# Reordered evacuations, swapped probability buffers, a longer output tail and a moved remainder in a streamed four-layer trunk

## The reference

```
score = where(adm, sum_h w_h * relu(qi_h . ki), -inf);  idx = top_k(score, n_sel)
logits = q . k[idx] * HEAD_DIM**-0.5 + bias;  out = softmax(logits) . v[idx] @ w_o
# recurrent block
y = gelu(xn @ w_y + b_y);  xc = causal_dwconv(xn @ w_x + b_x) + conv_b
r, ig = sigmoid(xc @ w_r + b_r), sigmoid(xc @ w_i + b_i);  a = exp(-8 * r * softplus(-lam))
h_t = a_t * h_{t-1} + sqrt(1 - a_t**2) * ig * xc;  out = (h * y) @ w_out + b_out
# every layer, and one last norm
x = x + mixer(rmsnorm(x));  x = x + swiglu(rmsnorm(x))
```

## Time and profile before

| | |
|---|---|
| median of 3 executions | 1799.42 us (1798.11 to 1799.64) |
| the profiled execution | 1799.41 us, its span 1797.6 us |
| mean granted TensorE clock | 0.994 |
| PE busy | 1773.3 us (99%) |
| DVE, ACT, POOL busy | 1068.2 us (59%), 715.7 us (40%), 223.6 us (12%) |
| DMA | 216.96 MB, 121 GB/s |

### The profile page before, as it was taken

One profiled execution on the slowest core, in us unless ns is written; L12 is line 12 of the kernel. 1 busy time (PEld: TensorE's weight loads), 2 busy tenths in 40 slices (PEclk: granted clock), 3 DMA queues, 4 the chain that ended last, 5 costly groups with the idle time before them and its releaser, 6 DMA issues.

```text
span 1797.6 us, 27817 instructions
## 1 busy us (share of the span) xinstructions
PE 1773.3 (99%) x10014; PEld 1736.3 (97%) x10014; DVE 1068.2 (59%) x1848; ACT 715.7 (40%) x1139; POOL 223.6 (12%) x266
## 2 busy tenths in 40 slices
PE   9999999999999999999999999999999999999997
PEld 8988999999999999999999999999999889999997
DVE  7976855544587755554476655554458756555533
ACT  5366433333368433333222343333323554333331
POOL 5000300001235400001100200000140004000010
PEclk9999999999999999999999999999999999999998
DMA  8311333333333433334433333333454113433341
GB/s 304 121 36 60 111 123 122 123 119 128 122 111 106 132 129 118 124 114 136 139 117 117 119 118 125 121 124 120 136 187 161 48 48 95 133 132 118 129 141 59
DMA packets 63844, 216.96 MB, mean 121 GB/s; under 512 B 7153, under 2 KB 8769, under 8 KB 63521
## 3 DMA queue, kind: packets, MB, share of 16 engines
q1 hardware_dynamic: 59520, 202.25, 34.1%
q0 software_dynamic: 3280, 12.12, 2.2%
q10 hardware_dynamic: 976, 1.70, 0.3%
HBM read 212.38 MB, written 3.66 MB: 120 GB/s over the span
## 4 chain that ended last, share of the span: by engine, by line
PE 90%; DVE 6%; ACT 3%; issue 1%; DMA 0%; DVEq 0%; ACTq 0%
PE bank L705 26%; PE bank L704 26%; PE bank L703 26%; DVE w_lo L1308 2%; PE bank L903 1%; PE bank L859 1%; PE bank L880 1%; PE bank L861 1%; PE bank L860 1%; PE bank L922 1%; ACT w_hi L1026 1%; PE bank L886 1%; DVE work_b L1465 0%; DVE cv L1641 0%; PE bank L929 0%
## 5 line engine op out<-in xcount | busy, mean ns | idle before, releaser
L1308 DVE TENSOR_TENSOR w_lo<-raw,w_hi 128x1024 fp32r<-128x1024 f32 x382 | 490.4, 1288 | 312.3 <-ACT w_hi L1026 310.7
L703 PE MATMUL bank<-a_hi,w_hi 128*128 128x400 f32 (+2 forms) x1936 | 673.3, 348 | 1.1 <-DVE w_lo L1308 1.1
L704 PE MATMUL bank<-a_lo,w_hi 128*128 128x400 f32 (+2 forms) x1936 | 666.0, 344 | 0.0
L705 PE MATMUL bank<-a_hi,w_lo 128*128 128x400 f32 (+2 forms) x1936 | 665.3, 344 | 0.0
L1026 ACT ACTIVATE w_hi<-raw 128x1024 fp32r<-128x1024 f32 x382 | 399.9, 1052 | 345.7 <-PE bank L705 339.2
L703 PEld LDWEIGHTS bank<-a_hi,w_hi 128*128 128x128 f32 (+1 forms) x1936 | 362.5, 187 | 5.2 <-issue 1.2
L705 PEld LDWEIGHTS bank<-a_hi,w_lo 128*128 128x128 f32 (+1 forms) x1936 | 364.8, 188 | 0.6
L704 PEld LDWEIGHTS bank<-a_lo,w_hi 128*128 128x128 f32 (+1 forms) x1936 | 362.7, 187 | 2.6
L705 PE MATMUL bank<-h_hi,w_lo 128*128 128x400 f32 (+1 forms) x704 | 240.8, 342 | 0.0
L704 PE MATMUL bank<-h_lo,w_hi 128*128 128x400 f32 (+1 forms) x704 | 240.1, 341 | 0.0
L703 PE MATMUL bank<-h_hi,w_hi 128*128 128x400 f32 (+1 forms) x704 | 239.2, 340 | 0.0
(11 more groups left out here) (251 smaller groups left out, 1770.3 us busy)
## 6 DMA issues: line engine op xcount, KB each, us to landing
raw<-in_w_all SPq DMA_DIRECT2D x382, 512.0 KB, 3.5
bias_p<-rel_scratch POOLq DMA_DIRECT2D x2, 2176.0 KB, 11.0
k_s<-in_ck_t POOLq DMA_DIRECT2D x4, 512.0 KB, 8.6
v_c<-in_cv POOLq DMA_DIRECT2D x2, 1024.0 KB, 15.9
ki_s<-in_cki_t POOLq DMA_DIRECT2D x4, 256.0 KB, 5.4
x<-in_x_t SPq DMA_DIRECT2D x2, 400.0 KB, 6.4
x<-in_x_t ACTq DMA_DIRECT2D x2, 400.0 KB, 6.9
out_v_t<-v_f POOLq DMA_DIRECT2D x2, 400.0 KB, 5.0
```

What stands on the lines that cost most here:

```text
L703: pe.matmul(out, wh, hi[:, kc, c0:T], start=(first and n == 0), stop=False)
L704: pe.matmul(out, wh, lo[:, kc, c0:T], start=False, stop=False)
L705: mm = pe.matmul(out, wl, hi[:, kc, c0:T], start=False, stop=(last and n == len(blocks) - 1))
L1308: nc.vector.tensor_tensor(w_lo[:, s, :], raw[:, s, :], w_hi[:, s, :].bitcast(F32), ALU.subtract).then_inc(lo_ready, 1)
```

## The change

Six edits:

1. Where an attention core begins, DVE does `queries_out(2)` right behind `values_out`, then two `take(1)` in place of three, then `queries_out(3)`. The `split` for u0+12, the third `take(1)` and `mask_made(1)` move into the loop (steps 0, 2 and 3), and the rounds of `take(2)` and `mask_made(2)` come one step later.
2. `buffer_of` swaps the two probability buffers of gp = 1 (and in both cores the first group of gp = 1 now gets buffer 0), and ACT waits for u0+17 only where it writes buffer 1.
3. `WO_TAIL` is 9 and no longer 6: nine blocks of w_o stand behind the last step. The other 23 are spread over the same steps as 26 were.
4. In the recurrent layer the eight `low` move from POOL to DVE.
5. POOL's remaining `tap`s stand one behind the other.
6. `TAIL_BUSY`: five matmuls of 128 columns, of which nothing is read, stand ahead of each `last_sq` wait at the end.

```diff
-WO_TAIL = 6
+WO_TAIL = 9
+def buffer_of(a, g):
+    return (g - len(GROUPS[a]) // 2 * GROUPS[a][g][0][1]) % 2
@@ PE, values; ACT, the copy to pt
-                    p = pt[gp][g % 2]
+                    p = pt[gp][buffer_of(a, g)]
-                    if gp:
+                    if gp and buffer_of(a, g):
                         act.wait_ge(unit_used, u0 + 17)
@@ PE, the end (twice, ahead of last_sq 1 and of last_sq 2)
+            for _ in range(TAIL_BUSY):
+                pe.matmul(bank[7][:, 0:128], ones[:], ones[:], start=True, stop=True)
@@ DVE, ahead of the core's loop
                 values_out()
-                for _ in range(3):
+                queries_out(2, done(11))
+                for _ in range(2):
                     take(1)
-                mask_made(1)
-                queries_out(2, done(11))
-                split(None, 0, u0 + 12 + AHEAD)
                 queries_out(3, done(12))
@@ DVE, in the loop
                     if n < N_IT[a]:
                         reduced(n)
+                    if n == 0:
+                        split(None, 0, u0 + 12 + AHEAD)
...
-                    if n in (3, 5, 7, 9, 11):
+                    if n == 2:
+                        take(1)
+                    if n == 3:
+                        mask_made(1)
+                    if n in (4, 6, 8, 10, 12):
                         take(2)
-                    if n == 12:
+                    if n == 13:
                         mask_made(2)
@@ POOL, recurrent
-                for what, m in [(tap, 0), (tap, 1), (tap, 2), (low, 0), (tap, 3), (low, 1), (tap, 4), (low, 2), (tap, 5), (low, 3),
-                                (low, 4), (tap, 6), (low, 5), (restart, 0), (tap, 7), (restart, 1), (low, 6), (low, 7),
-                                (restart, 2), (restart, 3)] + [(scale, m) for m in range(4)]:
+                for what, m in [(tap, m) for m in range(7)] + [(restart, 0), (tap, 7), (restart, 1), (restart, 2), (restart, 3)] + [
+                                (scale, m) for m in range(4)]:
@@ DVE, recurrent (low as on POOL before)
-                behind = [[], [(taps, 0)], [(taps, 1)], [(taps, 2)], [(taps, 3)], [(taps, 4)], [(taps, 5)], [],
-                          [(taps, 6), (rest, 0)], [(taps, 7), (rest, 1)], [(rest, 2)], [(rest, 3)], [(recur, 0)],
+                behind = [[], [(taps, 0)], [(taps, 1)], [(low, 0), (taps, 2)], [(low, 1), (taps, 3)], [(low, 2), (taps, 4)],
+                          [(low, 3), (taps, 5)], [(low, 4)], [(low, 5), (taps, 6), (rest, 0)], [(taps, 7), (rest, 1)],
+                          [(low, 6), (rest, 2)], [(low, 7), (rest, 3)], [(recur, 0)],
```

More of the change, by code:

```diff
@@ L72, in rec_unit @@
     return k, sum(1 for kd, _ in REC[:k] if kd != "g")
-WARM_UP = 24
+WARM_UP, TAIL_BUSY = 24, 5
 (P_NMIX, P_NFFN, P_NFIN, P_BY, P_BX, P_CW, P_CB, P_BR, P_BI, P_LAM, P_BO, P_CC) = (
@@ L593, in tap @@
                                        ALU.mult, ALU.add).then_inc(tap_ready, 1)
-                def low(m):
-                    pool.wait_ge(conv_hi, m + 1)
-                    pool.tensor_tensor(b_lo[:, m, :], xc[:, m, :], b_hi[:, m, :].bitcast(F32), ALU.subtract).then_inc(xc_fed, 1)
                 def restart(m):
@@ L1135, in copies @@
                     slot = n - (LAST[a][g] - len(GROUPS[a][g]) + 1)
-                    p, ps = pt[gp][g % 2], bank[4 + k % 2]
+                    p, ps = pt[gp][buffer_of(a, g)], bank[4 + k % 2]
                     act.wait_ge(tr_done, UB[a] + k + 1)
@@ L1674, in merged_low, with low @@
                     nc.vector.tensor_tensor(b_lo[:, m, :], y_b[:, m, :], b_hi[:, m, :].bitcast(F32), ALU.subtract).then_inc(fed, 1)
-                behind = [[], [(taps, 0)], [(taps, 1)], [(taps, 2)], [(taps, 3)], [(taps, 4)], [(taps, 5)], [],
-                          [(taps, 6), (rest, 0)], [(taps, 7), (rest, 1)], [(rest, 2)], [(rest, 3)], [(recur, 0)],
+                def low(m):
+                    dve.wait_ge(conv_hi, m + 1)
+                    nc.vector.tensor_tensor(b_lo[:, m, :], xc[:, m, :], b_hi[:, m, :].bitcast(F32), ALU.subtract).then_inc(xc_fed, 1)
+                behind = [[], [(taps, 0)], [(taps, 1)], [(low, 0), (taps, 2)], [(low, 1), (taps, 3)], [(low, 2), (taps, 4)],
+                          [(low, 3), (taps, 5)], [(low, 4)], [(low, 5), (taps, 6), (rest, 0)], [(taps, 7), (rest, 1)],
+                          [(low, 6), (rest, 2)], [(low, 7), (rest, 3)], [(recur, 0)],
                           [(recur, 2), (rest, 4), (rest, 5)], [], [(rest, 6), (rest, 7)],
```

## The result

The changed kernel takes 1787.91 us (median of 5 executions, 1787.87 to 1789.58); 1788.3 was forecast. The kernel before took 1798.11, 1798.18, 1799.42 and 1799.64 us in the same series, and once 2925.82, an execution that nothing on record explains and that is left out here. Against 1799.42, the median that the forecast started from, the gain is 11.5 us; against 1798.80, the median of the four, it is 10.9. The ratio on record is 0.9941, with an interval of 0.9925 to 0.9957.

The account below looks back on a forecast made before the run. PE bounds the kernel, busy 1773.3 of 1797.6 us, plus its idle places and clock losses. Gains 0.8 + 1.8 + 1.4 + 4.6 + 1.7 + 0 + 0.8 = 11.1 us from 1799.4 give 1788.3 us, range 1785.0 to 1794.5.

Parts of the forecast that it names:

- The rule of the Trainium skill that spoke against the edit: Recurrent layer: `low` on DVE would meet POOL's `cv`; four stretched cost 3.2 us more, a loss of about 1.5.
- the debt: Attention cores' beginnings: moved take, mask and w_lo, 2.5 us of DVE work, expected to eat about one microsecond in layer 0.
- Beginnings: Starts of both attention cores, evacuations first: gain 0.8 us in layer 0 and 1.8 in layer 3.
- the lead: Attention cores' beginnings: `logits(1)` comes 1.75 us earlier because `queries_out(3)` starts when PE delivers.
- Buffers: Second half of heads, swapped probability buffers: gain 1.4 us in layer 0 and 4.6 in layer 3.
- the nine blocks: Cores' ends: three more kept blocks cover nothing, gain 0, bounds -0.5 and 2.4; rival that they cover, chance 0.03.
- Recurrent layer: `low` moved to DVE: chain 1.72 us earlier, half clock behind the gates gone, output product wait grows; gain 1.7 us.
- End: Program's end: busy matmuls hold the clock, last pair takes half its 1.65 us; gain 0.8 us.
- The first, a fall behind the output product: Rival: the clock falls at the recurrent layer's longer second stall; price 1.5 us, 1789.8 us, chance 0.25.
- the x phase was relieved: Rival said not: recurrent layer's line 1645 stays at 1.13 us, DVE has 1.96 more; 1792.0 to 1793.2 us, chance 0.06.
- the debt didn't eat the lead: Rival said it would: moved work eats the whole lead in both cores; price 0.8 + 1.8, 1790.9 us, chance 0.13.
- the w_lo of u0+23: Rival: 6.4 us later in each core, it delays the ring's loads; 12.8 us, to 1801.1 us, chance 0.03.

Follow-up runs that it names:

- edit 2 alone: The kernel before with only the swapped probability buffers of gp = 1, ACT waiting for u0+17 only at buffer 1: 1792.25 us, ratio 0.9965.
- edit 6 alone: The kernel before with only the two sets of five busy matmuls at the end: 1797.12 us, ratio 0.9994.
- the runs with single edits: The kernel before with some edits only: edit 1 1795.24 us, edit 2 1792.25, edits 4 and 5 1796.98, edit 6 1797.12.
- edit 1: The kernel before with only the evacuations moved ahead of the top-k where the attention cores begin: 1795.24 us, ratio 0.9982.

## Why the steps held

**POOL beside DVE.** The changed kernel, with a subtraction on POOL that nobody reads, in the places that `low` had there.

```diff
+                def beside(m):
+                    pool.wait_ge(conv_hi, m + 1)
...
+                    pool.tensor_tensor(sq[:], xe[:, m, 0:T], xe[:, m, 4:T + 4], ALU.subtract).then_inc(beside_done, 1)
...
-                for what, m in [(tap, m) for m in range(7)] + [(restart, 0), (tap, 7), ...
+                for what, m in [(tap, 0), (tap, 1), (tap, 2), (beside, 0), (tap, 3), (beside, 1), (tap, 4), (beside, 2), (tap, 5),
+                                (beside, 3), (beside, 4), (tap, 6)] + [(restart, 0), (tap, 7), ...
```

> The changed kernel, but POOL does a subtraction of two SBUF inputs of 400 columns for each of x tiles 0 to 4 where it did the low half before; nobody reads the result. Theory: the last convolution step on DVE was slow because it ran beside POOL's instruction with two inputs; it goes back from 0.35 to about 1.1 us in five units, a unit of DVE takes 4.57 + 0.8 = 5.4 us, and PE's wait at the gates grows by some 3 us: 1790.5 to 1792.5 us. Rival: the step was slow because it read and wrote xc while POOL read the same tile; POOL's instruction here reads xe alone, so the step stays at 0.35 and the time at 1787.9 us.

Measured: 1790.29 us (1790.19 to 1790.48), 2.3 us more than the changed kernel. One unit on DVE in the changed kernel, with the same pair in an earlier unit, where POOL's `cv` doesn't run beside it, and then the same unit of this one with POOL's row:

```profile
494.17 1.34 DVE L1647 SCALAR_TENSOR_TENSOR cv<-xe,par,cv 128x424 f32<-128x424 f32 x2
...
501.13 1.22 DVE L1310 TENSOR_TENSOR w_lo<-raw,w_hi 128x1024 fp32r<-128x1024 f32 x1
...
502.81 0.57 DVE L1686 TENSOR_TENSOR b_lo<-xc,b_hi 128x400 fp32r<-128x400 f32 x1
503.29 1.70 DVE L1647 SCALAR_TENSOR_TENSOR cv<-xe,par,cv 128x424 f32<-128x424 f32 x2
505.03 0.50 DVE L1649 SCALAR_TENSOR_TENSOR xc<-xe,par,cv 128x272 f32<-128x272 f32 x1
505.45 0.35 DVE L1651 SCALAR_TENSOR_TENSOR xc<-xe,par,cv 128x128 f32<-128x128 f32 x1
505.71 1.22 DVE L1310 TENSOR_TENSOR w_lo<-raw,w_hi 128x1024 fp32r<-128x1024 f32 x1
```

```profile
502.49 1.21 DVE L1317 TENSOR_TENSOR w_lo<-raw,w_hi 128x1024 fp32r<-128x1024 f32 x1
...
504.66 1.71 DVE L1654 SCALAR_TENSOR_TENSOR cv<-xe,par,cv 128x424 f32<-128x424 f32 x2
506.40 0.98 DVE L1656 SCALAR_TENSOR_TENSOR xc<-xe,par,cv 128x272 f32<-128x272 f32 x1
...
507.56 1.21 DVE L1317 TENSOR_TENSOR w_lo<-raw,w_hi 128x1024 fp32r<-128x1024 f32 x1
```

```profile
505.88 1.20 POOL L604 TENSOR_TENSOR sq<-xe 128x400 f32<-128x400 f32 x1
```

The step beside POOL's instruction takes 0.98 us for 0.50, though the two write different tiles, POOL doesn't read xc, and of xe each reads another tile: it is the two engines at work at once, not the tile. The rival falls. My size was off: with `low` ahead of it on DVE, POOL's instruction now meets the step of 272 columns in four of the five units, and costs 0.5 us a unit (507.56 - 502.49 = 5.07 against 4.58), not 0.8; only in the first it meets the last step, which takes 0.94 us for 0.34. So the time came out 0.2 us under the range of the theory. PE's wait at the gates is 2.33 us again. POOL's one-input `cv` (0.70 us) stretches what it meets too: the pair of line 1647 takes 1.70 us beside it, 1.34 without it earlier in the phase, where the `cv` meets the step of 272 columns instead (0.82 for 0.50). The `low` on DVE, 0.57, ends before that `cv` starts in each unit that I looked at, so it meets neither. The rule of the Trainium skill that spoke against the edit ("GPSIMD Engine Reference", section "8. Key points": VectorE instructions with two SBUF inputs contend with GpSimd's) agrees in kind with these rows: the stretched DVE instructions read two tiles each. The contention would have turned the edit into a loss only if each `low` had been stretched by as much as the step that met POOL's `low`, and by its place in the order it isn't.

**The low half first.** The changed kernel, with DVE's last `low` of each core ahead of `half_out(7)`.

```diff
-                        if ends[k] + 1 == n:
+                        if ends[k] + 1 == n and k < 11:
...
                         if e + LAG_LO == n and OUT[a][g][1]:
                             low(g)
+                    if ends[11] + 1 == n:
+                        half_out(7)
```

> The changed kernel, but DVE takes the last group's low half of each attention core ahead of half_out(7), the x that waits for the last of the nine kept blocks. Theory: PE's 1.03 and 1.41 us of idle at the cores' ends are that x and the low half behind it; both go, 1.2 + 1.6 us from start to start, 1785.2 us. Rival: what PE waits for is the chain of ACT's high half and the exponentials; then the low half isn't ready earlier and the time stays 1787.9 us.

Measured: 1785.11 us (1784.88 to 1785.28), 2.9 us less; 2.8 was expected. DVE's timeline of this run at the end of layer 0's core:

```profile
167.04 0.57 DVE L1589 TENSOR_TENSOR x<-bank,x 128x400 f32<-128x400 f32 x1 [1.61 <-PE bank L859]
167.53 0.45 DVE L1580 TENSOR_TENSOR b_lo<-bank,b_hi 64x64 fp32r<-64x64 f32 x2
169.23 0.57 DVE L1589 TENSOR_TENSOR x<-bank,x 128x400 f32<-128x400 f32 x1 [1.25 <-PE bank L859]
```

The low half is done 1.2 us ahead of the x that it had to wait for, PE has no idle row at either core's end, and the rival falls. That proves the reading of the earlier trace rows: the wait was the order of two instructions on DVE, and nine kept blocks cover it no better than six.

**The same with six blocks.**

```diff
-WO_TAIL = 9
+WO_TAIL = 6
```

> The same order (low half ahead of half_out(7)), but six kept blocks and no longer nine. Theory: the kept blocks are cover for the last group's chain, and with the new order they decide something: six blocks are 3.2 us in layer 0 against nine's 4.8. ACT's last high half is ready some 3 us before PE's first wait in layer 0 of the kernel before, so six suffice in layer 0; in layer 3 the last group is a full one and I expect 0 to 0.8 us of idle: 1785.2 to 1786.0 us. Rival: kept blocks cover nothing in either order; then it equals the run with nine within 0.1 us.

Measured: 1784.81 us (1784.80 to 1784.84). My theory, that six would leave idle time in layer 3, falls; no idle row stands at either end. The rival isn't met to the letter either: the kept blocks cover nothing, but the two runs are 0.3 us apart and not 0.1, since the 0.3 us that nine blocks cost in layer 3's core come back here too.

**The debt of the moved top-k.** On the last kernel, the rounds later in the loop.

```diff
-                    if n == 2:
+                    if n == 5:
                         take(1)
-                    if n == 3:
+                    if n == 6:
                         mask_made(1)
-                    if n in (4, 6, 8, 10, 12):
+                    if n in (8, 10, 11, 13, 14):
                         take(2)
-                    if n == 13:
+                    if n == 15:
                         mask_made(2)
```

> The run with six blocks and the low half first (1784.8 us), and in the loop the rest of the top-k later: take(1) at step 5, its mask at 6, the rounds of take(2) at 8, 10, 11, 13 and 14, the mask at 15. Theory: PE's four waits of 0.34 to 0.4 us for reduced(n) in steps 4 and 6 are the debt of the moved work; the two that stand behind the take go, the w_lo's stay, and DVE has time in the wider steps from 8 on: 1784.1 us. Rival: the debt only moves to the steps before 16, which need mask_s, and the time stays within 0.2 of 1784.8 us or grows.

Measured: 1786.25 us (1786.22 to 1786.35), 1.4 us more. Of PE's four short waits the two behind the take are gone, as said, but both cores have a new one at the first mask_s (PE's timeline):

```profile
103.54 0.22 PE L883 MATMUL bank<-mask_s,sel_b 128*128 128x144 bf16 x1 [1.21 <-DVE nmx L1566]
...
1413.95 0.22 PE L883 MATMUL bank<-mask_s,sel_b 128*128 128x144 bf16 x1 [1.27 <-DVE nmx L1566]
```

The rival was right: the debt only moves, and five rounds in seven steps were more than DVE could hide there.

**The output product's chain.** On the six-block kernel with the low half first, DVE takes three of POOL's products y * h.

```diff
+                def merge(m):
+                    dve.wait_ge(tail, 3 * m + (5, 3)[m % 2])
+                    dve.wait_ge(gelu_ready, m + 1)
+                    nc.vector.tensor_tensor(y_b[:, m, :], y_b[:, m, :], qq[:, m, :], ALU.mult).then_inc(yh_dve, 1)
...
-                          [], [(merged_low, 0), (merged_low, 1)], ...
+                          [(merge, 1), (merge, 2), (merge, 3)], [(merged_low, 0), (merged_low, 1)], ...
```

Left out of the piece: POOL skips these three products, and ACT's high halves of the three wait for `yh_dve`.

> The run with six blocks and the low half first (1784.8 us), and in the recurrent layer DVE multiplies y by the recurrence for tiles 1 to 3, which POOL did in 1.27 us each. Theory: the chain of POOL's products, ACT's high halves and DVE's low halves is what PE waits for at the output product (0.39 and 1.16 us); DVE's three take some 0.5 us each, its w_lo there is no longer stretched to 2.0 us, and about 1.0 to 1.2 us go: 1783.7 us. Rival: ACT's gelus and high halves set the chain and POOL's products are hidden; then under 0.3 us go.

Measured: 1783.56 us (1783.55 to 1783.64), 1.25 us less than the kernel it is made from, and the fastest of all: 14.6 us under the 1798.20 of the kernel before in the same series, ratio 0.9916 (0.9899 to 0.9932), and 4.4 under the changed kernel. DVE's and PE's timeline of this run:

```profile
560.02 2.24 DVE L1688 TENSOR_TENSOR y_b<-y_b,qq 128x400 f32<-128x400 f32 x3 [0.60 <-ACT y_b L1196]
562.19 1.21 DVE L1315 TENSOR_TENSOR w_lo<-raw,w_hi 128x1024 fp32r<-128x1024 f32 x1
...
567.01 0.45 PE L703 MATMUL bank<-b_hi,w_hi 128*128 128x400 f32 x1 [0.83 <-DVE b_lo L1692]
```

The first wait (0.39) is gone, the second is 0.83 for 1.16. The w_lo that takes 1.21 us here took 2.03 beside POOL's products in the changed kernel:

```profile
563.43 2.03 DVE L1310 TENSOR_TENSOR w_lo<-raw,w_hi 128x1024 fp32r<-128x1024 f32 x1 [2.52 <-ACT w_hi L1028]
```

From the wait at the gates to the second one at the output product it is 567.01 - 525.29 = 41.72 us here and 568.27 - 525.55 = 42.72 in the kernel that it is made from. So the edit is worth 1.0 us, as the theory had it. The other quarter of a microsecond lies ahead of this stretch, most of it (0.17 us) ahead of layer 0's first `logits`, where the two kernels are the same; the two were measured in different series.

## Right, and how far

The forecast of 1788.3 was right to 0.4 us, and no step of its sum failed. Going through it:

- **Beginnings.** `logits(1)` came at 80.72 where 80.6 was worked out, and the debt ate 0.7 of the lead of 1.7, where one microsecond was expected. One reading on the way was off: DVE was to be through 1.2 us before PE's unit 12 ends, but by the earlier trace rows it is 77.66 + 1.12 = 78.78, 0.5 us before 79.32; the trace has two takes and `queries_out(2)` done at 78.72. It was still early enough, so nothing hung on it. In layer 3 the 2.2 us have two parts: the way to the first mask_s is 25.44 us in the kernel before, 24.27 with edit 2 alone, whose clock held, and 23.22 in the whole change, so the clock is 1.2 us of it and the idle places are 1.05. The forecast had 1.0 and 0.75.
- **Buffers.** From layer 3's first mask_s to the end of its core it is 69.16 us in the kernel before, 67.61 with edit 6 alone, whose clock held there, and 64.60 with edit 2 alone, which has no wait there. So the waits are 67.61 - 64.60 = 3.0 us and the half clock is 69.16 - 67.61 = 1.55: together the 4.6 of the forecast, to 0.05. The whole change gave 4.2, since the nine blocks take 0.3 back: forecast 0, measured -0.3, inside their bounds.
- **Recurrent layer.** DVE's pace is 4.57 to 4.59 us a unit (4.87 - 0.79 + 0.49 = 4.57 was implied), the last step 0.35. The wait at the gates is 0.45, those at the output product 1.55 in all. The sum of 1.7 holds, but its working went by a detour: it booked 1.5 for a half clock that goes and let the second wait grow by as much. The runs show that this half clock never had a price (42.70 us with it, 42.67 without).
- **End.** 0.91 for 1.65 us.
- **The rivals.** The first, a fall behind the output product, happened in two of the runs with single edits and in no profile of the changed kernel; its price was put at 1.5 and is 1.6. The others didn't happen: the x phase was relieved, the debt didn't eat the lead, and the w_lo of u0+23, later by design, delayed nothing that PE waited for (its waits for w_lo are 1.1 us in two places before and after).

Part of the agreement is luck. The forecast took the profiled execution of before as its base because it agreed with the median of three. It had four half-clock stretches; of the 11.1 us, 3.4 were clock, at layer 3's beginning, at its buffers and at the end, and it was not known that the kernel before loses these only in some executions, nor why the changed one would lose them in almost none. In the larger series the median of before is 1798.05 to 1798.37, and the gain 10.1 to 10.4 us. Without the clock the places give about 1.0 + 1.5 + 1.7 + 1.05 + 3.0 - 0.3 = 8.0.

## What to carry to other kernels

Where an engine is busy 99% of the time, list its idle rows one by one and ask of each which instruction stands ahead of the late one on the releasing engine: the cheapest gains here (2.9 us at the cores' ends, 4.2 at layer 3's buffers, clock included) were the order of two instructions and the choice of a buffer, not less work. Don't add up clock losses from one profile as if they belonged to their places; look at several executions' mean clock first, and ask whether a later wait would swallow the loss anyway. Work that is moved behind a late evacuation is a debt: it must fall due where the engine has room before the next deadline.

## What was not expected of the hardware

- The clock's fall behind a wait is not reproducible. Behind 2.1 us of idle at the gates it fell in two profiles (windows of 0.66 and 0.71) and held in two others with the same wait (1.00 with edit 1 and with edit 2 alone), and it held behind 2.33 us in the run with POOL's subtraction; behind 1.17 at the output product it fell in two profiles (0.70 and 0.77) and held in the others. Why the changed kernel and its successors are at 0.999 in nearly all executions, where single edits are not, was not settled.
- A DVE instruction beside a two-input one of POOL takes 0.98 for 0.50 (272 columns) or 1.13 for 0.34 (128 columns), w_lo 2.03 for 1.21 beside POOL's products; a one-input instruction of POOL costs DVE some 0.35 as well (1.70 for 1.34). So offloading to POOL is worth less than its row says, and moving a short instruction back to DVE can shorten DVE.
